# Attention output, recurrence and final projection in one program, with early products of seven heads and two products per chunk for the sample tile

## What is computed

```python
# end of layer 0 (attention), for prompt and sample
h = h + (o.reshape(B, L, ATT_WIDTH) * silu(z)) @ w_out
# layer 1: hn = rmsnorm(h, norm_w[1]); per head: recurrence over the tokens, giving o
o = o * rsqrt(mean(o * o, axis=-1, keepdims=True) + EPS) * gnorm
h = h + (o.reshape(B, L, REC_WIDTH) * silu(z)) @ rec_w_out
y = rmsnorm(h, final_norm_w)
```

## Time and profile before

| | us |
|---|---|
| runs of the kernel before, median of 3 | 1449.46 (1448.16 to 1450.64) |
| profiled execution, its own time | 1447.48 |
| its span in the trace | 1445.6 |
| PE busy in the span | 1380.3 (95%) |
| DVE, ACT, POOL busy | 904.1, 641.2, 674.3 |
| mean granted TensorE clock | 0.987 of full |
| attention output and its join to the recurrence | about 638 to 762 |
| recurrence, last projection done | 1301.1 |
| last product of the recurrence's last head | 1325.1 |
| final matmuls | 1338.5 to 1438.5 |

### The profile page before, as it was taken

The page is one execution under the profiler, slowest core; times in us unless marked ns, Lnnn a source line. Parts: engine busy times, 40 slices in busy tenths (PEclk is TensorE's granted clock), DMA queues, the critical chain, the costliest instruction groups (busy, mean ns, idle before and its releaser), DMA issues. The chain is left out here.

```text
span 1445.6 us, 21141 instructions
## 1 busy us (share of the span) xinstructions
PE 1380.3 (95%) x8028; PEld 1202.4 (83%) x8028; DVE 904.1 (63%) x1632; ACT 641.2 (44%) x1123; POOL 674.3 (47%) x469
## 2 busy tenths in 40 slices
PE   5999999999998999989999999999999999997998
PEld 5999845999986555558889999999999999996786
DVE  4211287999995877434558585858585858496232
ACT  4333365678774656531124443434343535253121
POOL 2466700564645766730024464747473738373000
PEclk9999999999999999989999999999999999998999
DMA  6221100223213310002231111111111111105321
GB/s 217 87 64 44 44 1 1 60 76 92 76 56 112 108 29 5 0 30 88 88 93 46 30 36 45 36 45 35 45 36 45 36 45 35 46 6 211 101 88 66
DMA packets 95315, 86.80 MB, mean 60 GB/s; under 512 B 5584, under 2 KB 83280, under 8 KB 95216
## 3 DMA queue, kind: packets, MB, share of 16 engines
q1 hardware_dynamic: 93584, 80.63, 18.2%
q0 software_dynamic: 1632, 4.82, 0.9%
HBM read 65.46 MB, written 19.97 MB: 59 GB/s over the span
## 5 line engine op out<-in xcount | busy, mean ns | idle before, releaser
L187 PE MATMUL bank<-hn_hi,rw_hi 128*128 128x352 f32 x768 | 251.1, 327 | 1.6 <-DVE hn_lo L177 1.6
L187 PE MATMUL bank<-hn_hi,rw_lo 128*128 128x352 f32 x768 | 247.6, 322 | 0.0
L187 PE MATMUL bank<-hn_lo,rw_hi 128*128 128x352 f32 x768 | 247.2, 322 | 0.0
L187 PE MATMUL bank<-hn_hi,w_hi 128*128 128x352 f32 x648 | 210.3, 324 | 3.3 <-ACT relu L676 2.5
L187 PE MATMUL bank<-hn_lo,w_hi 128*128 128x352 f32 x648 | 207.8, 321 | 0.0
L187 PE MATMUL bank<-hn_hi,w_lo 128*128 128x352 f32 x648 | 207.7, 321 | 0.0
L945 POOL TENSOR_SCALAR probs<-probs,low 128x128 f32<-128x128 f32 (+8 forms) x72 | 127.7, 1778 | 62.8 <-DVE low L1080 62.6
L187 PEld LDWEIGHTS bank<-hn_hi,rw_hi 128*128 128x128 f32 x768 | 144.7, 188 | 3.5 <-issue 3.0
L187 PEld LDWEIGHTS bank<-hn_lo,rw_hi 128*128 128x128 f32 x768 | 145.2, 189 | 0.0
L187 PEld LDWEIGHTS bank<-hn_hi,rw_lo 128*128 128x128 f32 x768 | 144.8, 189 | 0.0
L725 POOL TENSOR_TENSOR swapped<-swapped,sin 128x352 f32<-128x352 f32 x57 | 55.4, 971 | 186.4 <-ACT swapped L672 125.8
(11 more groups left out here) (231 smaller groups left out, 2965.3 us busy)
## 6 DMA issues: line engine op xcount, KB each, us to landing
rw_raw<-in_rec_w_in SPq DMA_DIRECT2D x32, 512.0 KB, 4.1
w_raw<-in_att_w_in SPq DMA_DIRECT2D x27, 512.0 KB, 4.0
q_rotated<-relu SPq DMA_DIRECT2D x24, 176.0 KB, 1.9
xin<-in_x_prompt SPq DMA_DIRECT2D x8, 512.0 KB, 4.0
wo_raw<-in_att_w_out SPq DMA_DIRECT2D x4, 1024.0 KB, 8.4
x_again<-in_x_prompt SPq DMA_DIRECT2D x8, 512.0 KB, 4.1
residual<-h_rows SPq DMA_DIRECT2D x8, 512.0 KB, 2.9
wf_raw<-in_rec_w_out SPq DMA_DIRECT2D x4, 1024.0 KB, 9.2
```

Of the source, the lines that this page charges most:

```text
L187: last = pe.matmul(out, l, r, start=n == 0, stop=n == len(passes) - 1)
```

## The change

One block, `out_recur_final`, holds the three stages; nothing meets between recurrence and final projection. The last projections' operands are split per tile into two pairs of buffers, `f_hi[t % 2]` and `f_lo[t % 2]`, which lie where the recurrence kept `log_f` and `log_decay`, and `k_to_end` and its rows. For tiles 0 and 1 the split and the first half's products (n = 0) come in two parts: heads 0 to 6 early (`EARLY = 7`), behind the last head's output products and ahead of its transposes; head 7 late. The other half and the other tiles have all eight heads at once. The gated heads are read back by tile, tiles 0 and 1 between weight pieces 1 and 2. The scratch of the final stage now begins where `levels` was. SP loads the final norm's weights and the first residual rows after the last head's output products.

For the sample tile `g_hi` (and `f_hi`) takes the 32 high columns in columns 0 to 31 and the 32 low columns in 32 to 63. Per chunk PE makes two matmuls, with the high and with the low weights. Rows 0 to 31 of the result belong to the high columns, rows 32 to 63 to the low ones. DVE adds the first to the residual straight from PSUM, ACT copies the second to `rows_s`, and DVE adds that in a second step. (So low x low is added as well, which is not in the three products.) Projections 0 and 1 of the recurrence wait for this second add (`h_ready`).

```diff
@@ output_product
+    if t == SAMPLE:
+        for k in range(KT):
+            for x in range(2):
+                last = pe.matmul(S["ps"][u % 4][:], g_parts[0][:, t % 2, k, :], w_parts[x][n][:, k, :],
+                                 start=k + x == 0, stop=k + x == KT)
+        return last
@@ attention_out, vector
                 for n in range(2):
+                    of, product_rows = slice(n * 512, (n + 1) * 512), ps[(2 * t + n) % 4][0:r, :]
+                    dve.wait_ge(out_ready, 2 * t + n + 1)
                     if t == SAMPLE:
+                        dve.tensor_tensor(xin[0:r, t % 2, of], product_rows, xin[0:r, t % 2, of], ALU.add).then_inc(added, 1)
+                        dve.wait_ge(added, n + 1)
                         dve.wait_ge(shifted, n + 1)
-                        product_rows = rows_s[:, n * 512:(n + 1) * 512]
-                    else:
-                        dve.wait_ge(out_ready, 2 * t + n + 1)
-                        product_rows = ps[(2 * t + n) % 4][0:r, :]
+                        product_rows = rows_s[:, of]
+                    dve.tensor_tensor(h[0:r, t % 2, of], product_rows, xin[0:r, t % 2, of], ALU.add).then_inc(h_ready, 1)
@@ recurrence
+    def final_hi(act, t, late):
+        of = f_heads(t, late)
+        act.wait_ge(dve_read, n_dve[at["out_T", RH - 1 if late else RH - 2, 2, None] + 1])
+        act.wait_ge(g_in[t], 16)
+        if t >= 2:
+            act.wait_ge(final_ready, 2 * (t - 1))
+        act.copy(f_hi[t % 2][:, of, 0:rows(t)], S["gT"][:, of, span(t)]).then_inc(f_hi_done, 1)
+
+    def final_lo(dve, t, late):
+        of = f_heads(t, late)
+        dve.wait_ge(f_hi_done, f_count(t, late))
+        low = f_hi[t % 2][:, of, DEC:2 * DEC] if t == SAMPLE else f_lo[t % 2][:, of]
+        dve.tensor_tensor(low, S["gT"][:, of, span(t)], f_hi[t % 2][:, of, 0:rows(t)].bitcast(F32),
+                          ALU.subtract).then_inc(f_lo_done, 1)
+
+    def final_product(pe, t, n, heads):
+        w_n = [x[:, :, n * 512:(n + 1) * 512] for x in (S["wf_hi"], S["wf_lo"])]
+        if (t, n) in ((0, 0), (0, 1)):
+            pe.wait_ge(wf_lo_dve if n else wf_lo_pool, 2)
+        pe.wait_ge(f_lo_done, f_count(t, heads.stop == RH))
+        kinds = ((f_hi, 0), (f_hi, 1)) if t == SAMPLE else ((f_hi, 0), (f_lo, 0), (f_hi, 1))
+        for k in range(heads.start, heads.stop):
+            for x, y in kinds:
+                last = pe.matmul(ps[(2 * t + n) % 4][:], x[t % 2][:, k, :], w_n[y][:, k, :],
+                                 start=k == 0 and x is f_hi and y == 0, stop=k == RH - 1 and y == 1)
+        return last
@@ recurrence, sync
             sp.wait_ge(acc_ready, RH * PER_HEAD)
-            for c, (ks, cols) in enumerate(weight_pieces()):
-                sp.dma_start(S["wf_raw"][:, ks, cols], w_final[:, ks, cols]).then_inc(wf_in[c], 16)
+            load_weights(0)
+            load_weights(1)
             sp.wait_ge(g_stored, 16 * STORED)
-            sp.dma_start(S["gT"][:, 0:STORED, :], g_dram[0:STORED].rearrange("h p t -> p h t")).then_inc(g_in, 16)
-            sp.wait_ge(g_in, 16)
+            load_gated(0)
+            load_gated(1)
+            load_weights(2)
+            load_weights(3)
+            for t in range(2, NT):
+                load_gated(t)
@@ recurrence, tensor
-                    pe.wait_ge(S["sample_read"], i + 1)
+                    pe.wait_ge(S["out_read"], 2 * SAMPLE + i + 1)
...
+            pe.wait_ge(acc_read, RH * PER_HEAD)
+            for t in range(2):
+                final_product(pe, t, 0, slice(0, EARLY))
             for g in range(3):
                 multiply("out_T", RH - 1, g)
@@ final_out, sync (now def sync)
+        S["wait_h_stored"](sp)
+        sp.wait_ge(*S["products_done"])
         sp.dma_start(fw[:], io["final_norm_w"].partition_broadcast(P)).then_inc(fw_in, 16)
@@ final_out, tensor (now def tensor)
-                pe.wait_ge(g_lo_done, t + 1)
...
-                    output_product(pe, S, (g_hi, g_lo), (w_hi, w_lo), t, n, u).then_inc(out_ready, 1)
+                final_product(pe, t, n, slice(S["EARLY"] if t < 2 and n == 0 else 0, RH)).then_inc(out_ready, 1)
```

More of the change, by code:

```diff
@@ L1109, in attention, with out_recur_final @@
     return dict(sync=sync, tensor=tensor, scalar=scalar, gpsimd=gpsimd, vector=vector)
-def out_and_recur(nc, S):
-    first, later = attention_out(nc, S), recurrence(nc, S)
+def out_recur_final(nc, S):
+    stages = [attention_out(nc, S), recurrence(nc, S), final_out(nc, S)]
     with nc.Block() as block:
@@ L1211, in split_lo @@
                 dve.wait_ge(g_hi_done, t + 1)
-                dve.tensor_tensor(g_lo[:, t % 2], gT[:, :, token_block(t)[0]], g_hi[:, t % 2].bitcast(F32),
+                low = g_hi[:, t % 2, :, DEC:2 * DEC] if t == SAMPLE else g_lo[:, t % 2]
+                dve.tensor_tensor(low, gT[:, :, span(t)], g_hi[:, t % 2, :, 0:rows(t)].bitcast(F32),
                                   ALU.subtract).then_inc(g_lo_done, 1)
@@ L1248, in split_hi @@
                     act.wait_ge(out_ready, 2 * (t - 1))
-                act.copy(g_hi[:, t % 2], gT[:, :, token_block(t)[0]]).then_inc(g_hi_done, 1)
+                act.copy(g_hi[:, t % 2, :, 0:rows(t)], gT[:, :, span(t)]).then_inc(g_hi_done, 1)
             split_hi(0)
@@ L1412, in recurrence, with f_count, f_heads @@
     wide_masks = levels[:, 0, 0:LEVELS * P]
+    f_hi = [Space(nc, at)(f"f_hi{x}", [P, KT, P], F32R) for x, at in enumerate(f_at)]
+    f_lo = [Space(nc, at + KT * P * 4)(f"f_lo{x}", [P, KT, P], F32R) for x, at in enumerate(f_at)]
+    EARLY = RH - 1
+    def f_count(t, late):
+        return t + 3 if t >= 2 else 3 + t if late else t + 1
+    def f_heads(t, late):
+        return slice(0, RH) if t >= 2 else slice(EARLY, RH) if late else slice(0, EARLY)
+    def final_hi(act, t, late):
[22 more added lines that the diff above has]
+        return last
+    S.update(final_hi=final_hi, final_lo=final_lo, final_product=final_product, final_ready=final_ready, EARLY=EARLY,
+             products_done=(product_ready, at["out", RH - 1, 2, None] + 1))
     def level_view(x, m):
@@ L1628, in scalar @@
                         read_product("k_T", p, g, kbT)
-                    for c in range(3):
+                    for c in range(2):
                         final_weights_hi(c)
+                    final_hi(act, 0, False)
+                    act.wait_ge(product_ready, at["state", RH - 1, 2, None] + 1)
+                    final_hi(act, 1, False)
+                    final_weights_hi(2)
                 for g in range(3):
@@ L1633, in scalar @@
             final_weights_hi(3)
+            for t in range(2):
+                final_hi(act, t, True)
         def gpsimd(pool):
@@ L1975, in _ @@
-        @block.gpsimd
-        def _(pool):
-            for t in range(NT):
-                norm_stats_pool(pool, stats, half, t, squares_ready, t + 1, mean_ready, rstd_ready)
+                    act.wait_ge(out_ready, u + 1)
+                    act.copy(rows_s[:, n * 512:(n + 1) * 512], ps[u % 4][DEC:2 * DEC, :]).then_inc(shifted, 1)
+            act.wait_ge(h_ready, 2 * t + 2)
+            if t:
+                act.wait_ge(squares_ready, t)
+            act.activation(junk[0:r], h[0:r, t % 2, :], ACT.Square,
+                           accum_out=stats[0:r, 0, t:t + 1]).then_inc(squares_ready, 1)
@@ L1981, in y_rows, with gpsimd @@
+    def gpsimd(pool):
+        for t in range(NT):
+            norm_stats_pool(pool, stats, half, t, squares_ready, t + 1, mean_ready, rstd_ready)
+    return dict(sync=sync, tensor=tensor, scalar=scalar, gpsimd=gpsimd, vector=vector)
 def y_rows(io, t):
```

189 lines of the change are left out of this document (90 added, 99 removed).

## The result

The changed kernel took **1432.88 us** (median; 1432.42 to 1434.15), the kernel before 1449.87 beside it (1448.16 to 1450.64): a ratio of 0.989, 95% interval 0.987 to 0.990. So it is faster by 17.0 us, or 1.1%. The forecast was 1432.6. The same kernel, run again on the chip of the first experiments, took 1436.19 (1434.57 to 1439.35), ratio 0.991 (0.989 to 0.993). All ten runs together have their middle at 1434.9; the gain is 13 to 17 us.

A forecast was written before the change was run, and what follows sets the result against it. The last chain was taken as bound by PE's final matmuls and when they may begin. End -16.3, tail +0.1, join -0.7 sum to -16.9 us; from the 1449.46 median, 1432.6 us, range 1429.5 to 1437.

The forecast's parts named there:

- (a): End of last head: 42 final matmuls run at once behind its output products, 9.5 us in time PE had idled.
- the rival of late inputs: End of last head: gated heads land only at 1323.6, gating 3.2 us worse, 1436 in all; chance 0.13.
- (b): End of last head: POOL's squares and all behind slip 0.65 us; second weight subtraction done at 1335.1.
- (c): Head 7's transposes wait behind early products, 2.4 us later but 1.2 long instead of 2.2; gating ends 1336.8, against 1335.83.
- (d): Start of late final products: only one head of two tiles left to split; PE begins at 1337.45 instead of 1338.49.
- (e): Late final products: 374 matmuls x 0.2267 = 84.8 us, ending 1422.2 against 1438.50, so -16.3 us for the end.
- That is gone if the clock holds: Start of late final products: 2.1 us of half clock vanishes; rival, clock falls at the end, +2.1, 1434.7, chance 0.15.
- (f): Final projection: no other engine becomes late, tightest at tile 2 with 0.8 us to spare; tail +0.1 us.
- The join: Attention projection to recurrence: 16 fewer matmuls not collected, PE idles 4.9 us, then half clock; net -0.7 us.
- if the clock falls a second time: Join between attention projection and recurrence: a second fall to half clock makes the net +0.5 to +1.3 us.
- The DVE adds: Join: new adds from PSUM with one SBUF operand take 0.69 us, hidden, or up to 2.9, moving the chain 0.8.
- the slower packets: Gated-head loads: packets cost the same whatever their length, so two tiles land at 1343; 1456 us in all; chance 0.03.

The follow-up runs named there:

- the shorter wait: Changed kernel, with ACT copying the sample rows after the first of three weight casts instead of after the third: 1432.02 us, ratio 0.989 to the kernel before.
- After: The changed kernel in its first runs and profile, against the kernel before: 1432.88 us, ratio 0.989.
- the other order: Changed kernel with last-head products and weight splits reordered; alone 1429.95 us, with copies and even tiles' buffers moved 1429.82, with those buffers 128 bytes later 1430.69.

## Why the prediction was right, and where it was not

The forecast said -16.9 us, the profiled executions differ by 15.1 (1447.48 and 1432.42) and the medians by 17.0. That forecast and median agree to 0.3 us is luck. By the traces the end stage gave 3.5 less than forecast, and the join and the tail what was forecast; 1.5 came from stretches in which nothing was changed (1.3 ahead of A, 0.6 from A to J, less 0.4 in the recurrence), and the other 2 us between traces and medians are the spread of the runs. Over all ten runs the gain is nearer to 15.

**(a) Early products: right.** 42 matmuls ran at once behind the last output product, 9.67 us until the transposes against 9.5. Their inputs were ready in time, and the rival of late inputs did not come: the loads of tiles 0 and 1, issued at 1299.96 and 1300.51, landed at 1309.49 and 1310.82, and ACT cast them from 1309.99 on, while the rival had the loads land at 1323.6. Undone, they cost 10.4 (traces), for 9.5 and part of the start.

**(b) Cover: right.** The squares slipped by 0.4 (2.63 for 2.24) where 0.65 was taken. The second weight subtraction ended 9.6 us after O, 10.0 by the working.

**(c) Transposes: right.** Gating began as soon as they allowed and ended at 11.98 after O, against 11.67 forecast.

**(d) The start was 0.45 too early.** Forecast 12.32 after O, measured 12.77. 0.3 of it is the later gating, the rest the two splits and their hand-overs (0.79 from gating's end to PE).

**(e) 374 x 0.2267 = 84.8 was mis-sized; they took 87.8.** Two terms. First, *the clock fell again*. "That is gone if the clock holds" had a rival with chance 0.15, argued away because nothing in the rows had fallen within 1.6 us of idleness. It fell in six of nine traces that have the pause of 1.9 (it held in those with three products in the final projection, with the shorter wait at the join, and with the even tiles' buffers 128 bytes on), and in none of the three in which the order fills the pause. After against the kernel with the shorter wait, which is alike from here on, 87.81 and 86.23, puts it at 1.6 us. The working counted PE's idle time alone. But the 1.2 us of transposes stand ahead of the pause. The three kernels with the other order keep the transposes, with 0.32 to 0.63 us of idleness ahead of them and none behind, and the clock held in all three; whether the pause by itself would make it fall was not tried. Nor does any run say why three of the nine held. Second, *the price per matmul*: 0.2267 was taken over from a stage in which all operands had the same place within 256 bytes. The new buffers of the even tiles do not, and 1.2 us were lost (86.23 to 85.04). With 85.04 for 84.8 the count itself is right. The sum: 1.6 + 1.2 + 0.2 + 0.45 makes the 3.5 that were missing.

**(f) No one late, tail +0.1: right.** No gap at tile 2 or later; F to the end +0.1.

**The join: right, in mechanism and size.** The save is not collected: PE waits 4.71 us for the add behind ACT's copies. The first product of the recurrence was forecast at 750.7, which is 13.2 after J (737.47 in the trace of before), and came 13.28 after it. The clock stood at half for 12 matmuls, as forecast. The third projection began 25.30 after J, where it had been 24.51 before: 0.8 later, forecast 0.4 to 1.2; and it ran at full clock, where it had been slow. Net, J to R, -0.8, where -0.7 was taken. The branch "if the clock falls a second time, +0.5 to +1.3" is real as well. Ten traces have the join as changed. Five show one fall of 9 to 12 matmuls, and against the 29.99 of before their J to R (28.91 to 29.28) is 0.7 to 1.1 less. Four show a second fall: two of them 0.8 and 0.9 more than before, two others 2.3 and 2.4 more, since the first fall held for 19 matmuls; that is beyond the branch. One shows a single long fall, of 15, and 0.1 less. Before itself has one trace.

**The DVE adds.** Of the new adds from PSUM the second ran beside POOL's subtractions (743.58 to 751.00) and took 0.67, as long as the first, which ran ahead of them. Those with two SBUF inputs took 1.35 and 2.14 there; at the end, with POOL idle, that kind took 0.69. So the lower bound holds. The Trainium skill, SBUF — State Buffer, section Who interferes with whom, says that a DVE instruction with one SBUF input does not contend with GpSimd and that one with two does. The trace agrees, with 0.67 against 1.35 and 2.14.

**Rivals.** The clock at the end came, priced at 2.1 and worth 1.6. Late inputs, the slower packets and products that are not early did not: the loads of the first two tiles had landed at 1310.82. The sample tile did not pay at the join by its count.

## What to carry to other kernels

When one stage ends in a chain of small steps on other engines, products of the next stage that need none of them belong behind the last product of this one: here 42 of them bought 10 of the 13 us in that stage. Nine of the 42, moved behind PE's own small step so that it no longer paused, together with a weight subtraction moved out of the chain, bought another 3. Price a saving at a place by the wait that ends last there: 16 matmuls fewer were worth 3.7 us at the end, and at the join nothing by their number, since PE only waited longer. When buffers are laid out anew, try the stationary operand at the same place within 256 bytes as the moving one; here one line was worth 1.2 us. And when one stretch is to show what an edit did, end it where the edit's effect ends: A to R, which takes in a stage that was not changed, would have shown 0.6 us of the clock as a gain of the join.

## What the runs showed of the hardware

The price of a float32 matmul of 128x512 depended on where its operands start against each other in SBUF: 0.2267 us at the same place within 256 bytes, 0.2325 at 128 bytes apart, in every tile of the final projection from the third on, and whichever tiles were moved. In the attention projection it was 0.2323 and 0.2271 in two halves whose weights start 96 and 0 bytes apart from the stationary operand; no run moved those. The clock fell to 1.2 GHz behind 1.2 us of transposes and 1.9 of idleness in six traces of nine, and held in three with the same rows ahead: the same code may pay 1.6 us or not. In after it was at 1.2 GHz from 1336.3 to 1339.7. A DVE add with one SBUF input took 0.67 us beside GpSimd's subtractions, adds with two took 1.35 and 2.14, where the same kind took 0.69 with GpSimd idle.
